# Gated heads: the forget gate's reciprocal in two halves, with a chunk's probabilities between them

## What is computed

```python
qh = jax.nn.silu(hq); vh = hi
f = lb + (1.0 - lb) * jax.nn.sigmoid(hf)          # forget gate
kh = 1.0 - f;  log_f = jnp.log(f)
# for each chunk of tokens
bcum = jnp.cumsum(gc, axis=2)                      # gc: log_f of the chunk
scores = jnp.einsum('bhtk,bhsk,bhtsk->bhts', qc, kc, exp(bcum_t - bcum_s))   # causal
o = scores @ vc + (qc * jnp.exp(bcum)) @ state
state = jnp.exp(b_end) * state + (kc * jnp.exp(b_end - bcum)).T @ vc
# then per head: rms(o) * hg_norm_w * silu(hg)
```

## Time and profile before

| | before |
|---|---|
| median of 3 executions | 4840.96 us (4838.16 to 4841.32) |
| the profiled execution, its own time | 4846.58 us |
| span of the profiled execution | 4844.8 us |
| mean granted TensorE clock | 0.994 of full speed |
| TensorE matmul busy | 4754.1 us, 98% |
| VectorE busy | 3168.4 us, 65% |
| ScalarE busy | 1583.0 us, 33% |
| gated heads | from about 750 to 1670 us of the span |

### The profile page before, as it was taken

How to read it: one execution, slowest core, us unless ns; L and a number is a source line. 1 busy time by engine, 2 the same in 40 slices (tenths; PEclk the granted TensorE clock), 3 DMA queues, 4 the chain that set the end, 5 groups by cost and what they waited for, 6 DMA issues and landing times. The chain is left out here.

```text
span 4844.8 us, 63431 instructions
## 1 busy us (share of the span) xinstructions
PE 4754.1 (98%) x23246; PEld 4103.9 (85%) x23246; DVE 3168.4 (65%) x4780; ACT 1583.0 (33%) x1534; POOL 1286.3 (27%) x543
## 2 busy tenths in 40 slices
PE   8999999999999999999999999999999999999998
PEld 6777778888888888888879999999999788888887
DVE  5677666777777612001168866667674798888888
ACT  3223333333333312122232268822222322222221
POOL 2333330000000033444434442266662111111110
PEclk9999999999999999999999999999999999999999
DMA  3233233222222344334233377799996898888885
GB/s 123 90 110 109 94 122 107 91 82 87 97 84 94 132 143 150 128 111 181 90 129 114 115 246 279 279 342 337 340 339 250 300 333 317 308 296 307 309 298 201
DMA packets 268688, 928.56 MB, mean 192 GB/s; under 512 B 38560, under 2 KB 129312, under 8 KB 190912
## 3 DMA queue, kind: packets, MB, share of 16 engines
q1 hardware_dynamic: 213312, 659.02, 38.7%
q0 software_dynamic: 55296, 268.53, 15.7%
HBM read 848.95 MB, written 78.51 MB: 191 GB/s over the span
## 5 line engine op out<-in xcount | busy, mean ns | idle before, releaser
L276 POOL TENSOR_TENSOR ring_low<-ring_raw,ring_high 128x2048 fp32r<-128x2048 f32 x155 | 725.3, 4679 | 2099.8 <-ACT ring_high L271 2099.8
L294 PE MATMUL rt_acc<-h_high,ring_high 128*128 128x384 f32 (+1 forms) x2304 | 791.5, 344 | 6.6 <-POOL ring_low L276 3.2
L295 PE MATMUL rt_acc<-h_low,ring_high 128*128 128x384 f32 (+1 forms) x2304 | 785.7, 341 | 0.0
L296 PE MATMUL rt_acc<-h_high,ring_low 128*128 128x384 f32 (+1 forms) x2304 | 785.3, 341 | 0.0
L271 ACT ACTIVATE ring_high<-ring_raw 128x2048 fp32r<-128x2048 f32 x337 | 645.0, 1914 | 399.7 <-PE mix_acc L296 266.2
L294 PEld LDWEIGHTS rt_acc<-h_high,ring_high 128*128 128x128 f32 x2304 | 433.6, 188 | 19.8 <-DVE h_low L314 5.0
L296 PEld LDWEIGHTS rt_acc<-h_high,ring_low 128*128 128x128 f32 x2304 | 433.4, 188 | 10.5
L295 PEld LDWEIGHTS rt_acc<-h_low,ring_high 128*128 128x128 f32 x2304 | 433.7, 188 | 9.4
L294 PE MATMUL hg_acc<-h_high,ring_high 128*128 128x512 f32 x1088 | 437.9, 402 | 1.7 <-DVEq L1275 1.6
L296 PE MATMUL hg_acc<-h_high,ring_low 128*128 128x512 f32 x1088 | 426.3, 392 | 0.0
L295 PE MATMUL hg_acc<-h_low,ring_high 128*128 128x512 f32 x1088 | 425.5, 391 | 0.0
(11 more groups left out here) (320 smaller groups left out, 9534.5 us busy)
## 6 DMA issues: line engine op xcount, KB each, us to landing
ring_raw<-u_tiles SPq DMA_DIRECT2D x128, 1024.0 KB, 5.1
ring_raw<-v_tiles SPq DMA_DIRECT2D x128, 1024.0 KB, 6.2
ring_raw<-w_hg SPq DMA_DIRECT2D x64, 1024.0 KB, 4.9
ring_raw<-w_ssd SPq DMA_DIRECT2D x48, 1024.0 KB, 6.3
ring_raw<-w_mix_s SPq DMA_DIRECT2D x32, 1024.0 KB, 5.5
ring_raw<-w_mix_h SPq DMA_DIRECT2D x32, 1024.0 KB, 4.8
gelu<-sent_gelu SPq DMA_DIRECT2D x128, 192.0 KB, 5.1
weights_gelu<-gelu SPq DMA_DIRECT2D x32, 768.0 KB, 8.1
```

Source lines behind the costliest of these rows:

```text
L276: nc.gpsimd.tensor_tensor(ring.low[:, slot], ring.raw[:, slot], ring.high[:, slot].bitcast(F32), ALU.subtract).then_inc(ring.low_ready, 1)
L294: nc.tensor.matmul(out, high[:, m], x_high[:, k, tokens], start=(k == 0), stop=False, skip_group_check=True)
L295: nc.tensor.matmul(out, high[:, m], x_low[:, k, tokens], start=False, stop=False, skip_group_check=True)
L296: last = nc.tensor.matmul(out, low[:, m], x_high[:, k, tokens], start=False, stop=(k == KT - 1), skip_group_check=True)
```

## The change

`take_f` is split in two functions. `start_f` holds the wait for the exponential, the addition and the reciprocal of the first 256 of 512 columns; `take_f` holds the reciprocal of the other 256 columns and the rest. `start_f` stands where `take_f` stood; `take_f` now stands behind `take_probs(p, 1)`, ahead of `next_state(p, 0)`.

```diff
-            def take_f(u):
+            def start_f(u):
 
                 dve.wait_ge(f_exp, u + 1)
                 vec.tensor_scalar(sg[:], f[:], 1.0, None, ALU.add).then_inc(acc_read, 1)
                 dve.wait_ge(acc_read, HG_TILES * u + 3)
-                chain.after(vec.reciprocal(sg[:], sg[:]))
+                vec.reciprocal(sg[:, 0:T // 2], sg[:, 0:T // 2])
+
+            def take_f(u):
+                chain.after(vec.reciprocal(sg[:, T // 2:T], sg[:, T // 2:T]))
                 vec.tensor_scalar(f[:], sg[:], lb[:, 1, ds(u, 1)], lb[:, 0, ds(u, 1)],
                                   ALU.mult, ALU.add).then_inc(f_ready, 1)
                 dve.wait_ge(f_ready, u + 1)
...
                 if comp:
                     take_probs(p, 0)
                 if proj:
-                    take_f(u)
+                    start_f(u)
                 if comp:
                     dve.wait_ge(turned, 2 * p + 2)
                     vec.tensor_copy(k_tok[:].rearrange("p c v -> p (c v)"), ps_k[:]).then_inc(turned_read, 1)
                     take_probs(p, 1)
+                if proj:
+                    take_f(u)
+                if comp:
                     next_state(p, 0)
                     take_probs(p, 2)
```

## The result

| | before | after |
|---|---|---|
| median | 4841.14 us (4 runs) | 4804.23 us (4 runs, 4803.33 to 4806.52) |
| profiled execution, its own time | 4846.58 us | 4803.33 us |
| ratio after to before | | 0.9924, 95% interval 0.9913 to 0.9936 |
| gated heads, first to last projection matmul | 747.5 to 1676.1 us | 747.0 to 1639.8 us |
| from one head to the next, from head 2 on | 55.14, three times 56.76 us | 53.03 us |

The account below looks back on a forecast made before the run. TensorE was taken to bound the kernel, waiting for VectorE before `L1193`. Waits 31.7 + clock drops 4.8 = 36.5 us off the profiled 4846.58 gave 4810.1; the median was forecast at 4804.5 us, range 4798 to 4815.

Parts of the forecast that it names:

- The wait and its price: TensorE's wait before `L1193`, chunk 2's scores, for chunk 1's probabilities: goes entirely, 15 x 2.11 = 31.7 us.
- The rival that counted 27.2 us by the matmul records: Wait before `L1193` counted too high, 27.2 us in all: 4813.8 us; no chance of its own given.
- Half a reciprocal: VectorE's reciprocal of 256 columns: 1.75 us, from a line through the lengths for 512 and 16 columns.
- the rivals at R = 2.3, 2.83 and 3.35: Half a reciprocal lasts R, VectorE late at chunk 3: 4825 us (0.10), no change (0.03), 4856.4 us (0.05).
- their formula: Change of a head's time when VectorE's lateness reaches TensorE at chunk 3: 2R - 5.67 us, R being half a reciprocal.
- The margin at chunk 2: Chunk 1's probabilities end before TensorE wants to load weights for chunk 2's scores, with 1.0 us to spare.
- Three drops of 1.61 us: Granted clock at 0.50 of full speed behind three of the waits before `L1193`; to go, about 4.8 us.
- The rival "drops stay": Clock drops in the gated heads stay or move, or unprofiled runs had none: only 31.7 us, 4809.3 us; chance 0.20.
- The cost of one more instruction: One more VectorE instruction in sixteen heads: 154 ns each, 2.5 us in all, costing TensorE nothing.
- The thinnest place: VectorE's 0.65 us hold before `low` of weights 3: takes 0.57 us of lateness, 0.08 us left; sign: under 0.15 us.
- Head 0: Head without probabilities: its reciprocal halves stand one behind the other, 0.15 us more, beside projections.
- The wait before `L1203`: TensorE's wait for chunk 3's probabilities: stays as before, 15 x 0.3 us.

## Why the prediction was right

- **The wait and its price.** 2.11 us a head was forecast from starts; the heads recur 55.14 - 53.03 = 2.11 us faster. The rival that counted 27.2 us by the matmul records fell. The cut at 448 confirms the way of counting: 0.17 us of wait at the load cost 0.25 there, as 2.03 us cost 2.11.
- **Half a reciprocal.** 1.75 us forecast, 1752 ns measured. With it the rivals at R = 2.3, 2.83 and 3.35 had no ground. The run with both pieces lengthened shows that their mechanism was real: at 3.42 us a piece it ends slower than before, by 0.82 us a head where their formula has 1.17.
- **The margin at chunk 2.** 1.0 us forecast, 0.99 measured, and 1.20 us more work in front of it made TensorE's load 0.25 us late.
- **The clock.** Three drops of 1.61 us were to go; no head of the change has any, in three profiles. The runs tie them to these waits more firmly than the prediction could. Behind waits of 2.02 to 2.05 us the clock was low 7 times in 28, and never behind the two of 1.7 us. With two waits of 1.45 and 2.35 us in close succession it was low in all 14 heads; the first head, with 1.17 and 2.29 us, had no drop. Behind waits of 0.5 to 1.6 us it was never low, in 60 of them. The rival "drops stay" fell for the profiled executions.
- **What is open about the clock.** The length of the wait at the load does not tell everything: each trace has two more waits of 1.98 and 2.00 us, where this stage and the next one start, and none of these 26 is followed by a drop. By the matmul records they are 1.6 us, against 1.84 us for those of 2.03. Why seven of 28 like waits have a drop and the others none is open, and so is whether one long wait or the sum of two close ones counts. Whether the unprofiled executions had the drops can't be seen directly. Beside the repeats the kernel before had a mean granted clock of 0.994 or 0.995 in 27 of 28 executions, and the change had 0.996 or 0.997 in 16 of 17; the mean does not say where in an execution the clock was low.
- **The cost of one more instruction.** The fixed term of an instruction is as the Trainium skill's page "VectorE: DVE Perf Modes" has it, in the section quoted in the prediction: 1752 ns is the line's value with 154 ns. Its advice against small pieces had no price here: cut in place, a head lost 0.02 us. The second piece starts 0.08 us before the first one ends, and `f` starts 3.55 us behind the first piece, against 3.54 behind the whole reciprocal.
- **The sum.** The prediction took fifteen equal waits, 31.7 us. The first of them, in the turn behind head 0, is only 1.69 us long in the profile before, and its head became 1.75 us shorter (54.95 to 53.20). So the waits give 14 x 2.11 + 1.75 = 31.3 us, the three drops 4.8, less 0.3 us for head 0: 35.8 us. The stage got shorter by just that (928.6 to 892.8). The medians say 36.9, and 38.1 and 37.9 in the repeats. The one to two microseconds beyond are open: they lie within what the kernel before varies by. The two profiled executions differ by 43 us, 7 of which lie behind the stage; in the two repeats of the change that later part was 2 to 4 us longer, so it varies without any change. That the median came within 0.3 us of the forecast is therefore in part luck: the forecast took the three drops of one profiled execution for the median of all, and a profile of the old order with the reciprocal cut in place has four.

Three smaller steps were off. **The thinnest place** was described as a hold of 0.65 us, all of it room. Of it some 0.12 us is VectorE's wait for its own query (`L1323`, later `L1326`): that much is left before `low` 3 in the runs where ScalarE is done by then (the reciprocal moved whole, more work behind chunk 1). So the hold ended at 0.21 us, where the prediction had named under 0.15 as a sign. VectorE in turn reached chunk 2 at 8.20 us behind the first half instead of 8.35, and the two nearly cancel: about 0.1 us was spare. **Head 0** was said to hide its 0.15 us beside projections: TensorE's wait before `L294` for `low` grew from 0.2 to 0.4 us there, and the first interval from 45.76 to 46.07 us; in the two repeats it was 45.90 and 46.31, so this is a few tenths of a microsecond, once. **The wait before `L1203`** stayed, as forecast, but the prediction let it pass for 0.3 us a head; it is worth 0.1.

## What to carry to other kernels

Look at which instruction's consumer is really late, and put in front of it only what it needs. Here the whole gain came of the order, and a cut was not needed; whether it is, the spare time at the next place tells. Work that is moved behind has to be followed to the next exposed place on its engine, and waits for an own result count as work, unless something independent stands between. A TensorE wait is priced by the starts of matmuls on either side, against the same products without a wait; the idle time that a row shows can be more or less than this price.

## What the runs showed of the hardware that was not expected

- What a wait at TensorE's weight load costs depends on how the load stands without it. Before `L1193` the load starts 0.11 us behind the one ahead and 0.08 us before that one's end, so waits of 0.17 and 2.03 us cost 0.25 and 2.11, 0.08 more than their length. Before `L1203` it runs 0.24 us ahead of its matmul, and a wait of 0.29 us cost about 0.1, 0.2 less. No run shows an added cost for starting again: from the load to `L294` it takes 1.27 us behind a wait of 2.03 us and 1.28 without one.
- The granted clock fell to its lower level of 1.2 GHz at 7 of 28 waits of 2.02 to 2.05 us, and behind none of 60 waits of 0.5 to 1.6 us. So the removed waits were worth more than their own microseconds: 36.1 instead of 31.3 us.
- A VectorE instruction that follows the one it depends on starts 0.19 us late and lasts 0.55 us (`f`); with an independent reciprocal between, it started without a gap and lasted 0.45. An instruction between does not always do it: behind chunk 1's probabilities, in the run with only `f` and `k` moved, `f` lasted 0.55 us again. The wait for an own result took 0.12 us before the copy `k_tok` and before `low` 3, which don't read that result.
